# Two transformer blocks on one core: order of the first loads, of the staging and of the gate copies, and the reciprocal root by Ln and Exp

## The reference

```python
# first block, each layer
h = x @ w_in[i]                       # queries, keys, values, index scores, gates
o_fox = softmax(q k / 8 + c_q - c_k, causal) v         # 6 heads, c = cumulative log forget gate
o_sb  = stick_breaking(q, k, v)                        # 5 heads
o_dsa = softmax over the 128 keys with the best index score; 5 heads, 1 key and value head
merged = g0 * (o_fox @ up_fox) + g1 * (o_sb @ up_sb) + g2 * (o_dsa @ up_dsa)   # g = sigmoid(gates)
x = layer_norm(ALPHA * x + merged @ w_out)
x = layer_norm(ALPHA * x + square(relu(x @ w_ff_in)) @ w_ff_out + sigmoid(x @ w_ple_gate) * (p @ w_ple))
# second block, each layer; then a final rms_norm
proj = rms_norm(x) @ w_in_2[l]
x = x + concat(nsa_attention * silu(z), rg_lru * silu(z), conformer_conv * silu(z)) @ w_out_2[l]

layer_norm: (x - mean) * rsqrt(var + eps) * g + b ;  rms_norm: x * rsqrt(mean(x * x) + eps) * g
```

## Time and profile before

| | |
|---|---|
| median of 3 runs | 2868.33 us (2866.03 to 2868.89) |
| the profiled execution | 2867.27 us, its span 2865.5 us |
| TensorE busy (matmuls) | 2721.0 us, 95% |
| VectorE, ScalarE, POOL busy | 51%, 40%, 37% |
| mean granted clock of TensorE | 0.981 |
| chain that ended last | TensorE 81%, VectorE 7%, ScalarE 4% |
| moved by DMA | 220.24 MB, 77 GB/s |

### The profile page before, as it was taken

One profiled execution on the slowest core, in us unless ns is written; L12 is line 12 of the kernel. 1 busy time (PEld: TensorE's weight loads), 2 busy tenths in 40 slices (PEclk: granted clock), 3 DMA queues, 4 the chain that ended last, 5 costly groups with the idle time before them and its releaser, 6 DMA issues.

```text
span 2865.5 us, 36041 instructions
## 1 busy us (share of the span) xinstructions
PE 2721.0 (95%) x12740; PEld 2058.4 (72%) x12740; DVE 1474.5 (51%) x2448; ACT 1141.3 (40%) x1979; POOL 1063.7 (37%) x430
## 2 busy tenths in 40 slices
PE   7998999999999989889999999999899999999998
PEld 5865656778888768566667788887687766787665
DVE  2066645672233220756455724232788764788754
ACT  2234434352223342434453522333436654337553
POOL 4331212434454334212123445444246522346612
PEclk9999999999999999989999999999999999999999
DMA  4220111222232213111112222322123211233201
GB/s 155 95 67 30 52 45 48 93 75 97 93 103 96 88 66 102 52 38 52 37 57 91 84 93 96 102 95 81 59 97 117 80 37 52 76 101 118 74 31 52
DMA packets 60884, 220.24 MB, mean 77 GB/s; under 512 B 6880, under 2 KB 7008, under 8 KB 60640
## 3 DMA queue, kind: packets, MB, share of 16 engines
q1 hardware_dynamic: 60192, 217.12, 22.8%
q10 hardware_dynamic: 576, 1.57, 0.2%
HBM read 216.57 MB, written 2.10 MB: 76 GB/s over the span
## 4 chain that ended last, share of the span: by engine, by line
PE 81%; DVE 7%; DVEq 4%; ACT 4%; issue 2%; POOL 1%; DMA 1%; ACTq 0%; SPq 0%; POOLq 0%
PE bank L380 22%; PE bank L382 21%; PE bank L381 21%; PE bank L496 3%; PE bank L523 3%; DVEq L2058 2%; PE bank L509 2%; POOL w_lo L406 1%; PE bank L843 1%; PE bank L709 1%; PE bank L499 1%; PE bank L1011 1%; PE bank L727 1%; PE bank L731 1%; DVE proj L1365 1%
## 5 line engine op out<-in xcount | busy, mean ns | idle before, releaser
L406 POOL TENSOR_TENSOR w_lo<-w_raw,w_hi 128x1024 fp32r<-128x1024 f32 x404 | 1012.6, 2516 | 1769.5 <-ACT w_hi L389 1754.5
L380 PE MATMUL bank<-x_hi,w_hi 128*128 128x512 f32 x2128 | 888.2, 417 | 68.3 <-DVE x_lo L2284 18.7
L381 PE MATMUL bank<-x_lo,w_hi 128*128 128x512 f32 x2128 | 838.5, 394 | 0.0
L382 PE MATMUL bank<-x_hi,w_lo 128*128 128x512 f32 x2128 | 838.3, 394 | 0.0
L389 ACT ACTIVATE w_hi<-w_raw 128x1024 fp32r<-128x1024 f32 x400 | 419.7, 1055 | 446.0 <-PE bank L382 433.8
L380 PEld LDWEIGHTS bank<-x_hi,w_hi 128*128 128x128 f32 x2128 | 405.0, 190 | 208.2 <-issue 94.1
L382 PEld LDWEIGHTS bank<-x_hi,w_lo 128*128 128x128 f32 x2128 | 405.1, 190 | 88.1
L381 PEld LDWEIGHTS bank<-x_lo,w_hi 128*128 128x128 f32 x2128 | 406.4, 191 | 82.0 <-issue 9.6
L380 PE MATMUL bank<-rhs_hi,w_hi 128*128 128x512 f32 (+1 forms) x656 | 254.5, 400 | 7.4 <-DVE rhs_lo L1436 7.4
L381 PE MATMUL bank<-rhs_lo,w_hi 128*128 128x512 f32 (+1 forms) x656 | 250.9, 392 | 0.0
L382 PE MATMUL bank<-rhs_hi,w_lo 128*128 128x512 f32 (+1 forms) x656 | 250.8, 391 | 0.0
(11 more groups left out here) (387 smaller groups left out, 3337.1 us busy)
## 6 DMA issues: line engine op xcount, KB each, us to landing
w_raw<-w SPq DMA_DIRECT2D x404, 512.0 KB, 3.4
ln_in<-x SPq DMA_DIRECT2D x1, 2048.0 KB, 7.9
out<-residual SPq DMA_DIRECT2D x8, 256.0 KB, 2.1
p_raw<-p ACTq DMA_DIRECT2D x2, 512.0 KB, 3.9
constants<-con SPq DMA_DIRECT2D x1, 455.0 KB, 3.1
cos<-cos SPq DMA_DIRECT2D x1, 256.0 KB, 3.6
sin<-sin SPq DMA_DIRECT2D x1, 256.0 KB, 3.6
params_b<-prm_b ACTq DMA_DIRECT2D x1, 256.0 KB, 2.6
```

Of the source, the lines that this page charges most:

```text
L380: nc.tensor.matmul(out, wh, xh, start=first, stop=False)
L381: nc.tensor.matmul(out, wh, xl, start=False, stop=False)
L382: S.last = nc.tensor.matmul(out, wl, xh, start=False, stop=last)
L406: S.nc.gpsimd.tensor_tensor(S.wl[s][:, :], S.raw[s][:, :], S.wh[s][:, :].bitcast(F32), ALU.subtract).then_inc(S.lo_ready[s], 1)
```

## The change

It does eight things.

- SP issues unit 0, a quarter of x, unit 1, the next quarter, and so on; constants, cos, sin, parameters and mask follow. VectorE casts and subtracts x tile by tile and casts the constants behind it.
- The first head pair of the forget attention is staged inside the index-score loop: ScalarE before steps 12 and 16, VectorE ahead of the sums.
- In `pairs_pe` the second fill of a pair stands ahead of the values of the pair before, in all three attentions.
- In the forget attention `round_gates` runs ahead of the next exponentials and not behind the copies.
- In the up projections tile 5 is issued alternately for the lower and the upper sum.
- ScalarE converts the finished output tiles for the up projections without waiting for the last one, and VectorE copies the last one out between the second and third subtraction.
- Every reciprocal root is Exp(-0.5 Ln(v + eps)) on ScalarE; the reciprocal on VectorE is gone. The table for both is preloaded behind the second block's attention.
- In the second block one Exp stands ahead of a Silu and not behind it.

```diff
 def sp_stream(S, sp, w_dram, groups):
-    for s in range(SLOTS):
-        sp.dma_start(S.raw[s][:, :], w_dram[s]).then_inc(S.raw_landed[s], 16)
...
@@ pairs_pe
         turn(n)
         if staged:
             scores(n + 1)
+        fill(n, 1)
         if n >= 1:
             values(n - 1)
-        fill(n, 1)
     values(N - 1)
...
@@ pairs_act
     exps(0)
     for n in range(len(pairs)):
+        if before:
+            before(n)
         if n + 1 < len(pairs):
             exps(n + 1)
         copy(n)
...
@@ ln_root_act
-    S.nc.scalar.activation(S.spare[:, :], S.eps[:, :], ACT.Sqrt)
+    S.nc.scalar.preload_act_table_set("natural_log_exp_and_others")
...
-    S.nc.scalar.activation(S.wk[2][:, :], S.wk[1][:, :], ACT.Sqrt, bias=S.eps[:, :]).then_inc(S.norm_std, 1)
+    S.nc.scalar.activation(S.wk[2][:, :], S.wk[1][:, :], ACT.Ln, bias=S.eps[:, :])
+    act.drain()
+    S.nc.scalar.activation(S.X[3][:, :], S.wk[2][:, :], ACT.Exp, scale=-0.5).then_inc(S.norm_std, 1)
...
@@ ln_dve (and the same in rms_dve, b_vector and at the end)
     dve.wait_ge(S.norm_std, n0 + 1)
-    nc.vector.reciprocal(S.X[3][:, :], S.wk[2][:, :])
...
@@ a_tensor, up projections
-                        (6, XD, True, False, 0, P), (7, XD, False, False, 0, P), (5, XD, False, True, 64, P),
-                        (5, XS, False, True, 0, 64))):
+                        (6, XD, True, False, 0, P), (7, XD, False, False, 0, P))):
...
+                for w, x, stop in ((S.wh, S.rh, False), (S.wh, S.rl, False), (S.wl, S.rh, True)):
+                    for e, out in enumerate((XS, XD)):
+                        m = nc.tensor.matmul(out, w[s][half(e), 5 * P:6 * P], x[half(e), 5 * SEQ:6 * SEQ], start=False, stop=stop)
+                m.then_inc(S.unit_done[s], 1)
...
@@ a_scalar
+        act.wait_ge(S.rope_done, (L + 1) * len(ROPE))
         for n, (b, h) in enumerate(idx_steps()):
+            if n in (12, 16):
+                fox_stage(n // 4 - 3, 0)
...
-        for e in range(2):
-            fox_stage(e, 0)
-        pairs_act(S, act, S.fox, L * 24, L * 12, fox_pairs(S), fox_after, depth=1)
+        pairs_act(S, act, S.fox, L * 24, L * 12, fox_pairs(S), fox_after, depth=1,
+                  before=lambda n: round_gates(FOX_FILL, n))
...
+        act.wait_ge(S.fox.out, (L + 1) * 3)
+        act.wait_ge(S.stk_oev, L * 5 + 6)
         for n, k in enumerate(OUT_ORDER):
-            act.wait_ge(S.dsa.out, (L + 1) * 3)
+            if k in DSA_TILE:
+                act.wait_ge(S.dsa.out, L * 3 + DSA_TILE.index(k) + 1)
...
@@ a_vector
+        dve.drain()
+        for e in range(2):
+            fox_rows(e, 0)
         dve.wait_ge(S.vt_done, (L + 1) * A_NVT)
...
-        for e in range(2):
-            fox_rows(e, 0)
...
-        out_tile(S.dsa, (L + 1) * 12, S.ps[3], DSA_TILE[2], half(1))
-
+        dve.wait_ge(S.dsa.o, (L + 1) * 12)
         for n, k in enumerate(OUT_ORDER):
+            if n == 2:
+                out_tile(S.dsa, (L + 1) * 12, S.ps[3], DSA_TILE[2], half(1))
...
@@ setup_sync
+    for s in range(SLOTS):
+        sp.dma_start(S.raw[s][:, :], T["w"][s]).then_inc(S.raw_landed[s], 16)
+        c = slice(2 * s * SEQ, 2 * (s + 1) * SEQ)
+        sp.dma_start(S.t[:, c], T["x"][:, c]).then_inc(S.x_landed[s], 16)
...
@@ setup_vector
-    nc.vector.tensor_copy(S.xh[:, :], S.t[:, :])
-    dve.drain()
     for k in range(KT):
+        if k % 2 == 0:
+            dve.wait_ge(S.x_landed[k // 2], 16)
+        nc.vector.tensor_copy(seq(S.xh, k), seq(S.t, k))
+        dve.drain()
+        nc.vector.tensor_tensor(seq(S.xl, k), seq(S.t, k), seq(S.xh, k).bitcast(F32), ALU.subtract).then_inc(S.x_ready, 1)
```

More of the change, by code:

```diff
@@ L536, in pairs_pe, with pairs_act @@
             scores(n + 1)
+        fill(n, 1)
         if n >= 1:
             values(n - 1)
-        fill(n, 1)
     values(N - 1)
-def pairs_act(S, act, Z, h0, p0, pairs, after, depth=2):
+def pairs_act(S, act, Z, h0, p0, pairs, after, depth=2, before=None):
     nc = S.nc
@@ L1560, in rms_root @@
     act.wait_ge(S.norm_var, norm(n0) * KT + KT)
[L1561 removed]
+    S.nc.scalar.activation(S.wk[2][:, :], S.X[1][:, :], ACT.Ln, bias=S.eps2[:, :])
+    act.drain()
+    S.nc.scalar.activation(S.X[2][:, :], S.wk[2][:, :], ACT.Exp, scale=-0.5).then_inc(S.norm_std, 1)
 def rms_act(S, act, n0):
@@ L2250, in b_vector @@
     dve.wait_ge(S.norm_std, norm(DEPTH) + 1)
-    nc.vector.reciprocal(S.wk[3][:, :], S.wk[2][:, :])
-    dve.drain()
     for j in range(KT):
-        stt(out=seq(S.res, j), in0=seq(S.res, j), scalar=S.prmB[:, PB_FINAL + j:PB_FINAL + j + 1], in1=S.wk[3][:, :],
+        stt(out=seq(S.res, j), in0=seq(S.res, j), scalar=S.prmB[:, PB_FINAL + j:PB_FINAL + j + 1], in1=S.X[2][:, :],
             op0=ALU.mult, op1=ALU.mult).then_inc(S.y_done, 1)
```

45 lines of the change are left out of this document (22 added, 23 removed).

## The result

The changed kernel took 2788.62 us (median of four runs, 2787.53 to 2794.87), the kernel before 2867.4 us. The ratio is 0.9725, 95% interval 0.9713 to 0.9736: 78.8 us less. I had forecast 2811.6 us with a range of 2798 to 2829. The sign was right; the gain was underestimated by 22 us (56.7 forecast), and the time lies outside the range.

What follows compares the result with a forecast made beforehand. TensorE was taken as the bound, its stops paid twice through the 1.2 GHz clock. 6 + 8.2 + 25.0 - 2.1 + 0 + 3.9 + 15.7 = 56.7 us off 2867.27 gave 2810.6, median 2811.6, range 2798 to 2829.

Steps and rivals of the forecast that it cites:

- The start: First input transfers and splits: weights and x quarters alternating let TensorE finish its first matmuls earlier, 6 us gained.
- Entry of the forget attention: First scores in two layers: staging inside the index-score loop brings the second scores earlier, 8.2 us gained, bounds 6.5 to 10.5.
- Gate units: Forget attention's filled-in gate matmuls: taking units before the exponentials removes six stops, 25.0 us gained with clock, less staging.
- The term for the clock: Behind the long gate stops: half of 17.3 us at the lower clock comes back, 8.65 us gained.
- Fill ahead of values: All three attentions: nothing moves in the middle, copies uncovered at the end of forget attention, 2.1 us lost, bounds 1 and 4.
- the 1.2 for staging: Forget attention: staging the next head pair ends about 0.3 us late, four times, 1.2 us lost, counted under gate units.
- Before the up projections: Stop ahead of the up projections: an earlier start in two layers, 1.9 us, plus 2.0 of clock; 3.9, bounds 1 and 9.
- POOL's hold: Ahead of the up projections: POOL's split holds VectorE's subtraction, so 1.9 us for two layers instead of 2.6 each.
- Half-height matmuls: Up projections: issuing upper and lower rows in turn changes nothing, 0 us, bounds 2.4 either way for 16 units.
- Root: Norms: logarithm and exponential replace RECIPROCAL, 2.57 us at five places plus 2.8 of short stops, 15.7 gained, bounds 12 and 17.
- the rivals: Clock does not return, 2822, chance 0.20; pairing new, 2801, 0.05; start no faster, 2817.6, 0.10; uncovered copies, 2875, 0.02.
- the one that came near 2801: Up projections: program order holds and pairing is new, saving three matmuls in 16 units, 10.7 us, 2801; chance 0.05.

Runs made afterwards that it cites:

- the run of one part alone: The kernel before, with the fill ahead of the values in the selected attention and the second block's attention only: 2848.59 us against 2868.9 beside it, ratio 0.993.
- the three-edit version: Changed kernel with values first in forget attention, last gate unit's split behind the eight conversions, x rounded on ScalarE between weight splits: 2779.77 us, 0.9693 to the kernel before.
- the delayed split: The three-edit version, with the last gate unit's split waiting for all eight VectorE subtractions and index-score fill tiles two together every fourth step: 2795.75 us.

## Why the prediction missed

**The start: right.** 7.3 us for 6, just over my 5.3 to 7. TensorE's first matmul came at 9.11 (forecast 11.0), the second stop ended at 14.56 (16.7). CAST is held by POOL as I had assumed from the COPY row: 2.52 us beside a split, 0.42 alone. My error was that VectorE gets its subtraction into the gap between POOL's splits: it did so at 8.37 and was done at 9.06, where my sum had 11.0.

```profile
5.67 2.35 POOL L404 TENSOR_TENSOR w_lo<-w_raw,w_hi 128x1024 fp32r<-128x1024 f32 x1 [5.21 <-ACT w_hi L1135]
5.77 2.52 DVE L2299 CAST x_hi<-ln_in 128x512 fp32r<-128x512 f32 x1 [4.22 <-DMA ln_in<-x]
...
8.37 0.69 DVE L2301 TENSOR_TENSOR x_lo<-ln_in,x_hi 128x512 fp32r<-128x512 f32 x1
...
9.11 0.80 PE L380 MATMUL bank<-x_hi,w_hi 128*128 128x512 f32 x1 [9.11 <-DVE x_lo L2301]
```

**Entry of the forget attention: right mechanism, undersized.** 11.0 by the medians, 10.6 by the starts, for 8.2. The chain is the one I named (score copy, row maximum, exponential, second scores); the stretch at 1.2 GHz behind it shrank too, which I had put in brackets and not in the sum: 17.0 us of it at the two entries before, 6.8 after.

**Gate units: idle right, clock undersized.** 17.5 of idle time to the digit. The term for the clock was 8.65; the runs show 12.8, and the 30.3 of both lies above my bound of 27. I had halved four stretches of one profile, 17.3 us in my windows, where its record of the granted clock has 20.5. The stretch behind a stop varies between executions, and the entry's stretch grows with the stops.

**Fill ahead of values: the step that failed.** I wrote "the total between two scores is unchanged, so in the middle nothing moves", "in the other two attentions there are two sets, and nothing is lost", and counted -2.1. The number of matmuls is unchanged, but not their neighbours: 0.2 us per step, 12.5 us over the 64 steps of the second block (the other 2.1 of its 14.6 come at the last step, 1.0 in layer 0, and with the clock) and 4 in the selected attention. A sign of it stood in my own: 1.22 us for one full matmul and three half-height pairs, 0.89 at 0.222 each. I had used those rows for another question and had not asked what the other 0.33 us are. In forget attention the size was off too: the order costs 4.1 us, where I had 2.1 and the 1.2 for staging.

**Before the up projections: 3.9 forecast, 7.4 measured** at this place. The stop itself went from 3.69 to 3.04, 0.65 for the 0.95 that I had put per layer, and by the run of one part alone the order of the fill does all of that; the new order of conversions and copy shows no gain of its own at this stop. About 4 us of the 7.4 are changes of shape in the selected attention, the rest the clock of layer 1 (one stretch of 6.8 us less), which scatters. POOL's hold, from the earlier trace rows, was right; the three-edit version only moves it to later subtractions.

**Half-height matmuls: right**, 0.

**Root: right**, 15.3 at its places for 15.7 (single stops 2.0 to 2.8). RECIPROCAL's 3.36 us went to an Exp of 0.60 us:

```profile
977.05 0.72 ACT L868 ACTIVATE work<-work,ln_eps 128x512 f32<-128x512 f32 x1 [1.06 <-DVE work L910]
977.84 0.60 ACT L870 ACTIVATE bank<-work 128x512 f32<-128x512 f32 x1
```

**The sum.** 23 us were missing between 56.7 and the 79.8 of the spans: 14.6 in the second block, 3.9 in forget attention, 3.5 around the up projections and 1.5 up to the last index score, less 0.4 at the roots. The range was too narrow because the term with "nothing moves" had no bounds: it rested on an argument and not on a row. Two of the eight edits, the conversions ahead of the up projections and the Exp ahead of a Silu, were not undone by themselves; what they are worth alone is not shown. None of the rivals described what happened; the one that came near 2801 did so by another rule, which was refuted.

## What to carry to other kernels

When matmuls change places, count changes between full-array, 64-row and 64-column matmuls along TensorE's queue, and put filled-in work next to work of its own shape: 0.2 us per separate stretch is invisible in a list of waits and was some 17 us here (12.5 and 4). Lay the start of the n-th instruction of two kernels side by side; it separates effects of 0.2 us per step that medians with 5 us of scatter don't show. When a stop gets shorter, add up all that TensorE waits for at the place: one of 3.04 us became three of 2.8 together. A wait put in front of a step also stands in front of all that is queued behind it: the delayed split gained 3.7 us and then lost 9.3.

## What the runs showed of the hardware

- TensorE's changes between full-array, 64-column and 64-row matmuls cost 0.14 to 0.20 us for three full matmuls put between the two others instead of behind full ones (4.40 us per step for 4.20), and about 0.3 us for six half-height ones put between full ones. The order of half-height matmuls among themselves makes no difference (1.22 and 1.24 us).
- Behind a stop the granted clock is at the lower level for 3.4, 6.8 or 10.2 us, and behind the same stop for different lengths in different executions; for one kernel the sum was 65.4 us in one profile and 80.7 in another, with spans 4.5 us apart.
- VectorE's CAST from fp32 to fp32r, which reads one tensor, is held by a POOL subtraction as a subtraction of its own is: 2.52 us for 0.42. A single-input rounding of 128x512 from fp32 was held too, 2.41 for 0.43.
